# The attention bias enters PSUM by an identity matmul, and maxima and exponentials read the scores in PSUM

## What is computed

```python
def memory_heads(xq, mem_k, mem_v, q_norm_g, k_norm_g):      # in mix_a and mix_b, 4 heads
    s = jnp.einsum('bthd,bmhd->bhtm', q, k) * M_HD ** -0.5
    p = jax.nn.softmax(s, axis=-1)                           # no bias, no mask

def diff_attention(q1, q2, k1, k2, v, lam, slopes):          # in mix_e
    bias = -slopes[:, None, None] * dist
    def probs(qb, kf):
        s = jnp.einsum('bhqd,bhkd->bhqk', qb, kf) * scale + bias
        return jax.nn.softmax(jnp.where(causal, s, -jnp.inf), axis=-1)
    p = probs(a1, k1) - lam * probs(a2, k2)
```

## Time and profile before

| | |
|---|---|
| device time, median of 3 runs | 1829.97 us (1824.23 to 1830.55) |
| profiled execution, its own time | 1829.21 us |
| its span | 1827.4 us |
| PE busy | 1688.5 us, 92% of the span |
| PEld busy | 1509.4 us, 83% |
| DVE busy | 1259.4 us, 69% |
| ACT busy | 946.3 us, 52% |
| DVE splits of weights, L89 | 629.7 us |
| ACT splits of weights, L80 | 539.9 us |
| mean granted clock of PE | 0.965 |

### The profile page before, as it was taken

One profiled execution on the slowest core, in us unless ns is written; L12 is line 12 of the kernel. 1 busy time (PEld: TensorE's weight loads), 2 busy tenths in 40 slices (PEclk: granted clock), 3 DMA queues, 4 the chain that ended last, 5 costly groups with the idle time before them and its releaser, 6 DMA issues.

```text
span 1827.4 us, 28948 instructions
## 1 busy us (share of the span) xinstructions
PE 1688.5 (92%) x10664; PEld 1509.4 (83%) x10664; DVE 1259.4 (69%) x2043; ACT 946.3 (52%) x1634; POOL 14.2 (1%) x20
## 2 busy tenths in 40 slices
PE   6999999899999999996899999878999989779997
PEld 5888897798888888875888889767998888579986
DVE  6666657577766776767577766867777566577765
ACT  5555453455545555555465544345665443356652
POOL 1000000000000000000000000000000000000000
PEclk9999999899999999998799999989999989989998
DMA  7454652265446554640155456204554543135442
GB/s 271 163 194 148 209 196 104 75 214 184 169 148 213 188 192 131 222 145 25 60 206 184 159 169 234 104 12 162 184 184 143 203 180 104 46 138 185 169 159 87
DMA packets 47360, 286.12 MB, mean 157 GB/s; under 512 B 5996, under 2 KB 6764, under 8 KB 23968
## 3 DMA queue, kind: packets, MB, share of 16 engines
q1 hardware_dynamic: 44640, 278.94, 43.4%
q10 hardware_dynamic: 2240, 5.19, 0.7%
q0 software_dynamic: 384, 0.68, 0.1%
HBM read 283.74 MB, written 1.05 MB: 156 GB/s over the span
## 4 chain that ended last, share of the span: by engine, by line
PE 82%; DVE 10%; ACT 5%; issue 2%; DMA 0%; ACTq 0%; DVEq 0%
PE ps_gemm L129 32%; PE ps_gemm L135 29%; PE ps_gemm L136 15%; DVE s_wlo L89 3%; ACT s_whi L80 2%; PE ps_gemm L805 1%; ACT s_work L816 1%; PE ps_sum L188 1%; PE ps_gemm L780 1%; DVE s_small L856 1%; DVE s_work L852 1%; PE ps_sum L805 1%; PE ps_sum L737 0%; ACT s_work L825 0%; DVE s_work L875 0%
## 5 line engine op out<-in xcount | busy, mean ns | idle before, releaser
L89 DVE TENSOR_TENSOR s_wlo<-s_wraw,s_whi 128x1024 fp32r<-128x1024 f32 (+3 forms) x608 | 629.7, 1078 | 425.7 <-ACT s_whi L80 425.6
L80 ACT ACTIVATE s_whi<-s_wraw 128x1024 fp32r<-128x1024 f32 (+3 forms) x608 | 539.9, 936 | 419.2 <-PE ps_gemm L136 213.4
L135 PE MATMUL ps_gemm<-s_xr,s_whi 128*128 128x512 f32 x1408 | 497.8, 398 | 5.4 <-DVE s_mem_v L691 3.1
L129 PE MATMUL ps_gemm<-s_xr,s_whi 128*128 128x256 f32 x2192 | 404.4, 287 | 10.3 <-DVE s_xr L249 7.9
L136 PE MATMUL ps_gemm<-s_xr,s_wlo 128*128 128x256 f32 x1408 | 395.6, 281 | 0.0
L135 PE MATMUL ps_gemm<-hid_r,s_whi 128*128 128x512 f32 x1056 | 375.1, 397 | 12.0 <-DVE s_wlo L89 12.0
L129 PEld LDWEIGHTS ps_gemm<-s_xr,s_whi 128*128 128x128 f32 x2192 | 346.0, 194 | 15.7 <-issue 10.8
L135 PEld LDWEIGHTS ps_gemm<-s_xr,s_whi 128*128 128x128 f32 x1408 | 264.9, 188 | 71.0 <-issue 6.0
L129 PE MATMUL ps_gemm<-s_xr,s_wlo 128*128 128x256 f32 x1096 | 311.8, 284 | 0.0
L136 PE MATMUL ps_gemm<-hid_r,s_wlo 128*128 128x256 f32 x1056 | 296.7, 281 | 0.0
L136 PEld LDWEIGHTS ps_gemm<-s_xr,s_wlo 128*128 128x128 f32 x1408 | 266.7, 189 | 0.1
(11 more groups left out here) (325 smaller groups left out, 1506.4 us busy)
## 6 DMA issues: line engine op xcount, KB each, us to landing
s_wraw<-in_stream_dram SPq DMA_DIRECT2D x178, 1024.0 KB, 4.8
s_wraw<-in_stream_dram SPq DMA_DIRECT2D x96, 704.0 KB, 4.1
s_wraw<-in_stream_dram SPq DMA_DIRECT2D x16, 768.0 KB, 4.3
s_wraw<-in_stream_dram SPq DMA_DIRECT2D x14, 512.0 KB, 3.3
s_room<-in_o_bias_dram ACTq DMA_DIRECT2D x1, 1536.0 KB, 9.7
s_room<-in_mem_dram SPq DMA_DIRECT2D x4, 256.0 KB, 4.5
s_x<-in_x_dram SPq DMA_DIRECT2D x1, 1024.0 KB, 5.4
s_room<-in_e_alibi_dram ACTq DMA_DIRECT2D x1, 1024.0 KB, 5.9
```

What stands on the lines that cost most here:

```text
L80: c.act.activation(c.whi[:, slot, s], c.wraw[:, raw, s], ACT.Copy).then_inc(c.hi_ready, 1)
L89: last = c.dve.tensor_tensor(c.wlo[:, slot, s], c.wraw[:, raw, s], c.whi[:, slot, s].bitcast(F32), ALU.subtract)
L129: last = pe.matmul(out, a, b, start=start and i == 0, stop=stop and i == 2, skip_group_check=skip)
L135: pe.matmul(bank.rearrange("p (a t) -> p a t", t=T), w_hi, x_both, start=start, stop=False)
```

## The change

Every job with a bias or a mask gets it by matmuls ahead of its scores: the identity times the bias, with start=True, and the score matmuls add to it (start=False). In mix_b and mix_e these are two float32r matmuls of 512 columns, and the identity, the mask and the slopes are first rounded to float32r by ACT, into buffers that lie over the originals. In mix_o the bias stays float32, in matmuls of 512 and 256 columns. The tables of slopes are multiplied by 8 on the host (the square root of the head's width), since the scale now comes after the bias. DVE reduces straight from PSUM, and the move L850/L852 goes. ACT reads the scores from PSUM, scales them inside the exponential and writes c.ss. The semaphore scores_taken goes: each wait of PE for it becomes one for exp_ready of the same job. The wait of DVE for a free slot of c.ss (values_done) passes to ACT, and the wait for the bias tables of mix_o from DVE to PE. The maximum is scaled in the small step that follows it.

```diff
-def scores_pe(c, job, n, bank, part=None):
...
+def scores_pe(c, job, n, bank):
+
+    for first, ident, bias in job.bias:
+        cols = bias.shape[1] if len(bias.shape) == 2 else bias.shape[1] * bias.shape[2]
+        out = bank[:, first:first + cols]
+        if len(bias.shape) == 3:
+            out = out.rearrange("p (h w) -> p h w", w=bias.shape[2])
+        c.pe.matmul(out, ident, bias, start=True, stop=False, skip_group_check=True)
+    for first, width, pairs in job.scores:
         for a, (q, k) in enumerate(pairs):
...
+            last = c.pe.matmul(bank[:, first:first + width], q, k, start=a == 0 and not job.bias, stop=a == len(pairs) - 1,
+                               skip_group_check=bool(job.bias))
+    last.then_inc(c.scores_ready, 1)
...
-def exps_act(c, job, n):
+def exps_act(c, job, n, bank):
     c.act.wait_ge(c.max_ready, n + 1)
-    s = n % 3
+    if n >= 3:
+        c.act.wait_ge(c.values_done, n - 2)
+    s, w = n % 3, job.width
...
-        e = c.ss[:, s, h * job.width:(h + 1) * job.width]
-        last = c.act.activation(e, e, ACT.Exp, bias=c.small[:, s, 16 + h:17 + h], accum_out=c.small[:, s, 32 + h:33 + h])
+        last = c.act.activation(c.ss[:, s, h * w:(h + 1) * w], bank[:, h * w:(h + 1) * w], ACT.Exp, scale=job.scale,
+                                bias=c.small[:, s, 16 + h:17 + h], accum_out=c.small[:, s, 32 + h:33 + h])
...
-    if job.bias is None:
-        ins = dve.tensor_scalar(v, src, job.scale, None, ALU.mult)
-    else:
-        ins = dve.scalar_tensor_tensor(v3, src.rearrange("p (h w) -> p h w", w=w), job.scale, job.bias, ALU.mult, ALU.add)
-    ins.then_inc(c.scores_taken, 1)
-    dve.wait_ge(c.scores_taken, n + 1)
...
+    dve_step(c, cnt, dve.tensor_reduce(m, bank[:, 0:job.cols].rearrange("p (h w) -> p h w", w=job.width), AX, ALU.max))
+    if job.sink is None:
+        dve.tensor_scalar(nm, m, -job.scale, None, ALU.mult).then_inc(c.max_ready, 1)
+        return
+    dve_step(c, cnt, dve.scalar_tensor_tensor(m, m, job.scale, job.sink, ALU.mult, ALU.max))
+    dve_step(c, cnt, dve.tensor_tensor(sd, job.sink, m, ALU.subtract))
...
+def rounded_act_copy(c, twin, v):
+
+    c.act.activation(twin, v, ACT.Copy).then_inc(c.rounded, 1)
...
@@ attention_pe: ahead of S(2), and ahead of S(n+3)
-    pe.wait_ge(c.scores_taken, cnt.job + 1)
+    pe.wait_ge(c.exp_ready, cnt.job + 1)
...
-            pe.wait_ge(c.scores_taken, n + 2)
+            pe.wait_ge(c.exp_ready, n + 2)
...
@@ mix_a_pe (mix_b_pe in the same way)
-    pe.wait_ge(c.scores_taken, n + 1)
+    pe.wait_ge(c.exp_ready, n + 1)
...
@@ mix_b_act: between the sines and the exponentials of the memory jobs
+    act.wait_ge(c.b_in, 16 * 5)
+    rounded_act_copy(c, c.ident_r[:, :], c.ident[:, :])
+    rounded_act_copy(c, b.mask_r, b.mask)
...
@@ mix_e_pe: ahead of S(0)
-    pe.wait_ge(c.scores_taken, cnt.job)
+    pe.wait_ge(c.exp_ready, cnt.job)
+    pe.wait_ge(c.rounded, 4)
     scores_pe(c, jobs[0], cnt.job, c.score_banks[cnt.job % 2])
...
@@ mix_e_act: behind the splits of units up to 9, ahead of the exponentials
+    act.wait_ge(c.e_tables_in, 16 * 5)
+    rounded_act_copy(c, e.alibi_r, e.alibi.rearrange("p h t -> p (h t)"))
+    rounded_act_copy(c, e.mask_r, e.mask)
     act.wait_ge(c.e_lambda_dots, 1)
...
@@ dilated_jobs
+            bias = [(i, c.ident[:, :], table[:, b0 + i:b0 + min(i + BANK, 6 * P)]) for i in range(0, 6 * P, BANK)]
```

More of the change, by code:

```diff
@@ L840, in maxima_dve, with banked_bias @@
 def maxima_dve(c, cnt, job, n, bank):
[L842 removed]
+    dve, s, h = c.dve, n % 3, job.heads
     dve.wait_ge(c.scores_ready, n + 1)
[L844 to L848, removed]
[L849 to L860 removed]
+    m, nm, sd = (c.small[:, s, a:a + h] for a in (0, 16, 48))
+    dve_step(c, cnt, dve.tensor_reduce(m, bank[:, 0:job.cols].rearrange("p (h w) -> p h w", w=job.width), AX, ALU.max))
[4 more added lines that the diff above has]
+    dve_step(c, cnt, dve.tensor_tensor(sd, job.sink, m, ALU.subtract))
+    dve.tensor_scalar(nm, m, -1.0, None, ALU.mult).then_inc(c.max_ready, 1)
+def rounded_act_copy(c, twin, v):
+    c.act.activation(twin, v, ACT.Copy).then_inc(c.rounded, 1)
+def banked_bias(c, view, heads, w):
+    per = BANK // w
+    return [(i * BANK, c.ident_r[:, :], view(i * per, per)) for i in range(heads // per)]
 def divide_dve(c, cnt, job, n):
@@ L936, in attention_act @@
 def attention_act(c, cnt, jobs, after=None):
-    exps_act(c, jobs[0], cnt.job)
-    exps_act(c, jobs[1], cnt.job + 1)
+    for i in range(2):
+        exps_act(c, jobs[i], cnt.job + i, c.score_banks[(cnt.job + i) % 2])
     for i, job in enumerate(jobs):
@@ L975, in memory_jobs @@
                    [(c.mem_v[:, mt, h * P:(h + 1) * P], 2 * h + mt) for mt in range(2)]) for h in range(4)]
-        jobs.append(Job(4, T, 1.0, None, scores, values, (slice(0, P), c.mem_y, 4, tt * P)))
+        jobs.append(Job(4, T, 1.0, [], scores, values, (slice(0, P), c.mem_y, 4, tt * P)))
     return jobs
@@ L1457, in window_jobs @@
         w = P * (blk + 1)
-        mask = b.mask[:, T - w:T].unsqueeze(1).to_broadcast([P, 2 * pairs, w])
+        mask = b.mask_r[:, T - w:T].unsqueeze(1).to_broadcast([P, BANK // w, w])
+        bias = banked_bias(c, lambda h, n: mask, 2 * pairs, w)
         for i0 in range(0, 8, pairs):
@@ L1466, in window_jobs @@
                                    [(b.v[:, kt, r * B_HD:(r + 1) * B_HD], h * (blk + 1) + kt) for kt in range(blk + 1)]))
-            jobs.append(Job(2 * pairs, w, B_HD ** -0.5, mask, scores, values, (slice(0, P), i0, pairs, blk * P),
+            jobs.append(Job(2 * pairs, w, B_HD ** -0.5, bias, scores, values, (slice(0, P), i0, pairs, blk * P),
                             sink=b.sinks[:, 2 * i0:2 * i0 + 2 * pairs]))
@@ L1498, in mix_b_pe @@
     pe.wait_ge(c.hn_used, cnt.hn)
-    pe.wait_ge(c.scores_taken, n)
+    pe.wait_ge(c.exp_ready, n)
     scores_pe(c, jobs[0], n, c.ps_s)
     unit(2)
-    pe.wait_ge(c.scores_taken, n + 1)
+    pe.wait_ge(c.exp_ready, n + 1)
     scores_pe(c, jobs[1], n + 1, c.ps_s)
@@ L1729, in latent_jobs @@
         q = slice(blk * P, (blk + 1) * P)
-        mask = e.mask[:, T - w:T].unsqueeze(1).to_broadcast([P, heads, w])
+        mask = e.mask_r[:, T - w:T].unsqueeze(1).to_broadcast([P, BANK // w, w])
+        bias = banked_bias(c, lambda h, n: mask, heads, w)
         for h0 in range(0, 8, heads):
@@ L1736, in latent_jobs @@
                       for h in range(h0, h0 + heads)]
-            jobs.append(Job(heads, w, E_SCALE, mask, scores, values, (slice(0, P), h0 // 2, heads // 2, blk * P)))
+            jobs.append(Job(heads, w, E_SCALE, bias, scores, values, (slice(0, P), h0 // 2, heads // 2, blk * P)))
     return jobs
@@ L2249, in sb, with twin @@
             return ctx.enter_context(nc.sbuf_tensor("s_" + name, [P, cols], dt))
+        def twin(name, cols, rounded):
+            at = -(-nc.sbuf_base // 32) * 32
+            first = sb(name, cols)
+            return first, nc.alloc_sbuf_tensor_at("s_" + name + "_r", [P, rounded], F32R, offset=at)
         def cube(t, b):
@@ L2349, in build @@
         c.scores_ready = sem("scores_ready")
-        c.scores_taken = sem("scores_taken")
         c.max_ready = sem("max_ready")
         c.exp_ready = sem("exp_ready")
+        c.rounded = sem("rounded")
         c.probs_ready = sem("probs_ready")
```

41 lines of the change are left out of this document (22 added, 19 removed).

## The result

Twenty runs of each kernel on one chip: before 1826.49 us (median), after 1830.89 us. The ratio is 1.0025 with a 95% interval of 1.0013 to 1.0037, so the change costs 4.6 us (2.4 to 6.8). A second timing, of twelve runs, gave 1.0023. The forecast said +7.9 us: the sign was right, the size too large. As a time it said 1837, which is 6.2 us too long: 2.7 of them because I counted from the one profiled execution, 1829.21, and 3.5 from the size of the change. The measured time is inside the range (1826 to 1848) but outside of the 1834 to 1841 to which I gave half of the chances; it lies between rival B (1826) and rival A (1833). The profiled execution of the changed kernel took 1831.70 us, its span 1829.9 (before 1829.21 and 1827.4).

The account below looks back on a forecast made before the run. PE was taken to bound the kernel (82% of the chain), with three engines in a ring in the attention. Terms 3.7 - 2.6 + 0.5 + 6.3 + 0 = +7.9 us on 1829.21 gave 1837, range 1826 to 1848.

Parts of the forecast that it names:

- rival B: Not slower: DVE's move ended the ring in every job; rings gain 7.3 us, -3.4 in all, 1826; chance 0.15.
- rival A: The clock holds in the two stalls: mix_a 2.1, mix_e 4.2, rest as forecast; +4.2, 1833; chance 0.13.
- mix_a: Second memory job's scores wait 2.5 us for job 0's exponentials: +2.1, plus 1.6 for clock; ends 2.1 and 3.7.
- mix_b, memory jobs: Scores 1.2 us later, but PE's 2.58 us wait for division and 1.6 of low clock vanish: -2.6, upper end 0.
- mix_b, attention: Job 2's scores behind job 0's exponentials, later scores sticking out, shorter maxima and exponentials: +0.5, ends -1 and +4.
- mix_e, up to its ring: PE stands 4.1 us for ACT's copies behind its splits, then runs at low clock: +6.5; 4.4 with clock up.
- mix_e, ring: Cold scores of job 1 +0.85, maxima -1.2, later scores, shorter exponentials: -0.2 net, ends -1 and +3.
- mix_o: First scores 1.28 longer by float32 bias, first maxima 0.95 shorter, kept clock pays about one bias: 0, ends -1 and +4.
- rival D: Bias matmul not single-pass: a pair takes 1.7 instead of 0.45, adding 7 on some six ring jobs; 1844; chance 0.04.
- one M: Maxima step of a job on DVE, 1.2 us shorter without the move, credited in the rings of mix_b and mix_e.
- S(2) behind E(0): mix_b's attention: job 2's scores start when job 0's exponentials end, 850.8 instead of 847.12; job 0's values +1.6.
- Rival C: Low clock through the rings: a PE gap per job, scores and bias at 1.2 GHz; +12 more, 1846; chance 0.18.

## Why the forecast was right and wrong

Means over the profiles named above, in us; the mix_a row is from the eight with the wait and the twelve without.

| term | forecast | measured |
|---|---|---|
| mix_a | +3.7 | +4.2 (2.2 wait, 2.0 clock) |
| mix_b, memory jobs | -2.6 | -3.0 (41.9 to 38.9) |
| mix_b, attention | +0.5 | -1.7 (47.8 to 46.1) |
| mix_e, up to its ring | +6.5 | +6.0 (23.2 to 29.2) |
| mix_e, ring | -0.2 | -1.8 (42.5 to 40.6) |
| mix_o | 0 | -0.1 |
| sum | +7.9 | +3.6; timed +4.6 and +4.2 |

Everything outside of these stages, from the start of the span to its end, adds up to 1555.5 us in the mean before (four profiles, 1554 to 1558) and 1555.5 after (three, 1553 to 1557), so no cost shows there. With the mean of all twelve profiles of the changed rings in place of three, mix_b's attention is -1.1, mix_e's ring -2.0, and the sum +4.0.

**Right.** The three terms in which a wait can be pointed at. Mix_e: the copies behind the splits make PE stand 4.04 us (4.1 forecast), S(0) cold costs 1.4 (1.7), and moving the copies undoes it. Mix_a: S(1) behind E(0), 2.58 us of wait as computed; the clock fell behind it in five profiles of eight, so the upper end was the right mean by luck as much as by reason. In the other three it held there, as rival A has it, but fell 15 us later; and in mix_e the S(0) behind the stall was slow in every profile that has the stall. Rival A did not come in any profile as a whole. Mix_b's memory jobs: the 1.0 us at S(1) is repaid by T(0)'s vanished wait and the clock behind it (the two parts that I gave, 1.3 and 1.6, make 2.9 and not the 2.6 of the sum; 3.0 was measured). The pair of bias matmuls takes 0.54 to 0.57 at full clock (0.45 forecast), float32 1.29 to 1.40 (1.28); rival D was wrong. Exponentials of 256 columns start 0.46 apart (0.45 forecast).

**Wrong.** The two rings of mix_b and mix_e, by 2.2 and 1.6 us (1.6 and 1.8 with all twelve profiles), beyond the lower end of -1 that I gave each, if only just in mix_b. They are nearly the whole of the error of the sum. The step that failed is the relief of DVE: I credited one M (1.2 us) to each ring, and 0.6 for the exponentials in mix_b, because V(3) waits for ACT in the earlier trace rows. The runs without bias matmuls show what reading PSUM without the move is worth against the kernel before: 47.8 - 44.1 = 3.7 in mix_b, 42.5 - 38.7 = 3.8 in mix_e, 38.0 - 32.2 = 5.8 in mix_o. Twice what I credited in mix_b, three times in mix_e, six times in mix_o, for 18 jobs 0.74 us each out of 1.22 or 0.96 removed. With the bias matmuls in place it is 3.5, 0.7 and 1.4. So in mix_b I credited 1.8 where the runs show 2.9 to 3.7, whichever way one counts and with three or all twelve profiles. In mix_e the credit is too small only without the bias matmuls; with the move kept it is the other side that fails, since the bias matmuls cost nothing there (40.4 and 42.3 against 42.5) where I had added cold and late scores. One wait behind ACT does not mean that DVE's time before it is free. In the timeline of before, ACT's copy for V(3) lies behind E(4) (873.58), this behind the output of V(2) (872.12), and V(2) behind S(5) and T(2), which had waited for DVE's D(2), and D(2) behind the move of M(3):

```profile
863.34 1.22 DVE L852 SCALAR_TENSOR_TENSOR s_work<-ps_gemm,s_room 128x1024 f32<-128x1024 f32 x1
...
866.72 1.23 DVE L875 TENSOR_TENSOR s_work<-s_work,s_small 128x1024 f32<-128x1024 f32 x1
...
868.00 1.12 PE L796 MATMUL ps_t<-s_ident,s_work 128*128 128x128 f32 x4 [3.16 <-DVE s_work L875]
...
872.12 1.14 PE L805 MATMUL ps_gemm<-s_work,s_room 128*64 128x128 f32 x16
...
873.58 0.20 ACT L813 ACTIVATE s_small<-s_small 128x4 f32<-128x4 f32 x1
```

I had read the last wait of the chain and not the one before it.

The other side: the bias matmuls, on top of that, cost 2.0 in mix_b, 1.9 in mix_e and 5.8 in mix_o. In mix_o I had 1.28 for one bias and 0.95 for one move. Counted from the kernel without the move, both are 5.8 for six jobs, and the two errors cancel; with the move kept they are 1.3 and 1.4, close to what I had. The term came out right, and which of the two reasons it was is a matter of order. S(2) behind E(0) made V(0) 2.5 us later where I had 1.6, which is repaid by the end of the ring.

Why the clock is higher in all rings (0.77 to 0.89, 0.82 to 0.92, 0.91 to 1.00) is open: it rises without the bias matmuls (0.88, 0.86 and 1.00) and with the move kept (0.83, 0.96 or 0.87, 1.00), so each half goes with it and the cause is not shown. Rival C, low clock through the rings, did not come; its 1846 is also a slip, since 12 more than the forecast is 1849, beyond my range. Rival B had the sign of the rings right and twice their size (7.3 us gained, 3.6 measured): without bias matmuls 13.3 of the 20.4 us of moves came back, with them 5.6, so DVE's move was not the end of the ring in every job.

The Trainium skill, page "VectorE: DVE Perf Modes", section on the TRN2 errata, adds fixed cycles for VectorE on PSUM; by my estimate from its figures each reduce would be 0.065 us longer. The rows disagree: 1.221 us in the mean of sixteen from PSUM, 1.220 of sixteen from SBUF. For ScalarE it has fewer cycles from PSUM, and the rows agree in sign: 0.473 against 0.499 us for 256 columns.

## What to carry to other kernels

Where three engines hand work round in a ring, don't price a removed step by the one wait that follows it: nearly every step is on the ring in some job. And don't price two changes to one ring apart and add them: here the same removal was worth 13.3 of 20.4 us on one side of the other change and 5.6 on the other side, and the same matmuls cost 2.0 or 9.7. When an operand has to be prepared by another engine, the place of that preparation in its queue matters more than its length: 2.2 us of copies cost 5.7 us behind two splits and nothing 15 us earlier. When a buffer is freed later, look for the stage with only one of them: in mix_a the wait came out as computed (2.58 us against 2.5).

## What was not expected of the hardware

The same wait of 2.58 us on PE, in the same place of the same code, was followed by half clock at once in some executions and by full clock in others: eight score matmuls took 3.78 us in one and 1.99 us in the other. Where it was full, it fell 15 us later, at a place where it also fell in three of twelve profiles without the wait. A single profile of a stretch with such a wait is uncertain by up to 3 us (to the spread; 1.7 to the projection). Whole runs scatter by more, with the wait or without: the changed kernel's twenty lie between 1825.6 and 1838.0, those of the kernel before between 1821.2 and 1832.2.

With exponentials of 128 columns from PSUM the duration in the profile grows along the row, from 0.37 to 0.46 us over sixteen of them in mix_b, while their starts stay 0.34 to 0.36 apart. The first two and the last of the changed kernel's first profile:

```profile
849.96 0.37 ACT L821 ACTIVATE s_work<-ps_s,s_small 128x128 f32<-128x128 f32 x1
...
850.32 0.36 ACT L821 ACTIVATE s_work<-ps_s,s_small 128x128 f32<-128x128 f32 x1
...
855.22 0.46 ACT L821 ACTIVATE s_work<-ps_gemm,s_small 128x128 f32<-128x128 f32 x1
```

The starts, not the durations, are what a sum should be made of.
